# Sample attention of a decoder step: the pages' keys turned by VectorE in 32x32 blocks, scores as nine rounds of four 32-row products

## The chip, the core and the metric

The kernel runs on one core of a Trainium2 chip. Its metric is the device time of one launch in microseconds (us), the median of three runs. A core has TensorE (matrix products out of SBUF into the eight banks of PSUM), VectorE, ScalarE, GpSimd and SyncE; each takes its instructions in order and waits on semaphores for the others. In this kernel SyncE issues nearly all DMAs.

## The reference

One inference step of a two-layer decoder. Each layer has a mixing part (a pooling branch and latent attention, MLA) and a channel part (a gated convolution FFN). It serves two groups with the same weights: a prompt of 512 tokens, and 8 sample sequences of 8 new tokens, each with a past of 2048 tokens that lies in a paged cache. What the change touches is the attention of the samples:

```
past = cache_latent[l][page_table].reshape(n_seq, n_pages * PAGE_SIZE, LATENT)   # 16 pages of 128 rows, 288 wide
keys = jnp.concatenate([past, latent], axis=1)
q_lat = jnp.einsum('bqhn,chn->bqhc', q_nope, lw['w_uk'])
s = einsum('bqhd,bkd->bhqk', [q_lat | q_rope], keys) * ATTN_SCALE    # masked, then softmax -> p
o_lat = einsum('bhqk,bkd->bqhd', p, keys[..., :KV_LORA])
o = jnp.einsum('bqhc,chv->bqhv', o_lat, lw['w_uv'])
```

A cached row is 256 latent values and 32 rope values, 288 in all. With 16 heads and 8 new tokens a sample sequence has 128 query rows, so the scores of one sequence are a product of 128 queries with 2048 + 64 keys over 288 values. All of it is fp32.

## The kernel before

Each layer goes through the projections (weights streamed by DMA and split in two parts by ScalarE and GpSimd), the prompt's attention head by head (16 heads), the sample attention sequence by sequence (b = 0 to 7, `NB`), the output projection and the FFN. Only the sample attention and its neighbours are of interest here.

Pages. `keys_of(b)` on SyncE loads the 16 pages of a sequence, one DMA each, into one of three buffers (`pages[b % 3]`, a key on each partition). Each DMA's address needs a number of the page table, so SyncE does a `value_load` (TENSOR_LOAD and two or three small instructions) ahead of each. `keys_of(0)` stands before the heads; `keys_of(1)` behind `k_asm` of head 15, `keys_of(2)` behind it, and each `keys_of(b)` from b = 3 waits for `spv` of b - 3, the end of the products with the values that read the buffer last.

Scores. The product needs the 288 values on the partitions, so TensorE turns the keys: `turn_rope(b)` (the 32 rope columns of 16 pages, four pages beside each other in the 32-column strips) and `turn_keys(b, g)` (g = 0 to 3, four pages at a time, two blocks of 128). VectorE and ScalarE copy what was turned from PSUM to `ropeT` and `keysT`. `rope_scores(b)` is four products of 32 rows beside each other (each on its own 32 partitions, into banks 0 to 3), `scores(b, g)` two products of 128 rows into bank g, and `new_scores(b)` the 64 new keys. VectorE takes the maximum of each bank as it is done, ScalarE the exponentials of all four banks (`sc`).

Values. `all_values(b)` turns the exponentials with TensorE (`turn_scores`), ScalarE and VectorE copy them to `pT`, and 16 products with the pages and one with the new keys (`newk`) fill bank 7 and raise `spv`. VectorE divides (`olat`, in `outputs(b)`), and TensorE turns that back one sequence later (`turn_output`).

The order is written out by hand: `all_scores(b)`, then `all_values(b - 1)`, so that the exponentials of b run beside the values of b - 1. `all_scores(0)` comes after the last head. The rope part of the queries, `qrs`, lies on partitions 0 to 31, and VectorE copies it to the other three groups of 32 behind head 3.

Of the kernel before, what the change touches and what calls it, by code (L numbers as in the profile page):

```python
# [25 lines left out]
ALU = mybir.AluOpType  # L26
ACT = mybir.ActivationFunctionType
# [56 lines left out]
def build(nc, A, O):  # L84
# [117 lines left out]
    keysT = [at("keysT0", [128, 2, 512], ckv_at), at("keysT1", [128, 2, 512], arena + 18432)]  # L202
    ropeT = [at("ropeT0", [128, 512], ckv_at + 4096), at("ropeT1", [128, 512], arena + 22528)]
# [88 lines left out]
    qlat_p, qlat_ev, qrs_ready = signal("qlat_p", 1), signal("qlat_ev", 1), signal("qrs_ready", 1)  # L292
# [41 lines left out]
    def keys_bank(b, g):  # L334

        return 1 if b == 0 and g == 0 else 4

    def rope_bank(b):

        return 0 if b == 0 else 6  # L340
# [7 lines left out]
    with nc.Block() as block:  # L348
# [3 lines left out]
        def _(sp):  # L352
# [19 lines left out]
            for l in range(DEPTH):  # L372
# [184 lines left out]
        def _(act):  # L557
# [69 lines left out]
            for l in range(DEPTH):  # L627
# [184 lines left out]
                def exponentials(b):  # L812
# [5 lines left out]
                    nc.scalar.activation(sc[:, 0:PAST], PS[:, 0:4, :].rearrange("p a b -> p (a b)"), ACT.Exp,  # L818
# [5 lines left out]
                def turned_scores(b):  # L824
                    for g in (0, 2):
# [3 lines left out]
                for b in range(NB):  # L829
                    keys(b, 0)  # L830
                    if b != 1:
                        keys(b, 1)
                    else:
                        act.wait_ge(newk_T.sem, newk_T.at(l, 1))
                        nc.scalar.activation(newk[:], PS[0:TS, 7, 0:KVL], ACT.Copy).then_inc(newk_ev.sem, 1)
                        keys(b, 1)
# [178 lines left out]
        def _(dve):  # L1015
# [105 lines left out]
            for l in range(DEPTH):  # L1121
# [1105 lines left out]
```

## Time and profile before

| | us |
|---|---|
| median of 3 runs | 2255.96 |
| lowest, highest | 2255.33, 2258.66 |
| the profiled execution | 2255.74 |
| its span | 2254.0 |
| TensorE busy | 2210.7 (98%) |
| VectorE busy | 1170.6 (52%) |
| ScalarE busy | 874.9 (39%) |
| GpSimd busy | 655.1 (29%) |

The profile is of one execution. A span of the trace counts from its first to its last instruction, and times in rows count from its start. In a row of instructions, `x8` counts records; an fp32 product is two records (two passes over its columns), a turn of 128x128 is one. PE is TensorE's products, PEld its weight loads, DVE is VectorE, ACT is ScalarE, POOL is GpSimd, and SPq is SyncE's issuing of DMAs. "Idle before" is the time an engine sat still ahead of a group and who released it.

### The profile page before, as it was taken

The page shows a single profiled execution, that of the slowest core. Times are in us where ns is not written, and L with a number is a line of the kernel's source. Part 1 is how long each engine was busy: PE and PEld are TensorE (multiplying, and loading weights), DVE is VectorE, ACT ScalarE, POOL GpSimd, SP SyncE. Part 2 cuts the span into 40 slices and gives each one's busy share as a digit, 9 for nine tenths or more (in the row PEclk, how much of TensorE's full clock was granted, in tenths as well). Part 3 has the DMA queues.
Part 4 walks back from the last instruction along what each step waited for, and adds up shares of the span by engine and source line. Part 5 has one row for each costly group of instructions (what it writes and reads, how often), then busy time and mean ns, then how long its engine had stood idle before and what let it go on. Part 6 is the DMA issues. An engine that isn't in the chain of part 4 may idle for free.

```text
span 2254.0 us, 42639 instructions
## 1 busy us (share of the span) xinstructions
PE 2210.7 (98%) x16239; PEld 1981.8 (88%) x16239; DVE 1170.6 (52%) x1831; ACT 874.9 (39%) x1815; POOL 655.1 (29%) x316
## 2 busy tenths in 40 slices
PE   7999999999999999999999999999999999999998
PEld 5899997667789999999988999966677999999998
DVE  4443753844346666651153717457443476666433
ACT  4223225832234555541132332366322355555322
POOL 0223433400022333333322334342000323333332
PEclk9999999999999999999999999999999999999999
DMA  9554332033333222235545333212332422222332
GB/s 302 170 145 100 85 85 66 19 109 108 85 130 91 79 84 84 84 109 167 173 126 176 83 97 83 79 43 63 97 108 57 156 70 83 79 80 83 87 85 84
DMA packets 338278, 230.69 MB, mean 102 GB/s; under 512 B 62732, under 2 KB 321605, under 8 KB 338140
## 3 DMA queue, kind: packets, MB, share of 16 engines
q1 hardware_dynamic: 336594, 226.37, 35.1%
q10 hardware_dynamic: 1546, 2.43, 0.4%
q8 instruction: 92, 1.51, 0.3%
q14 instruction: 46, 0.38, 0.1%
HBM read 223.15 MB, written 5.60 MB: 101 GB/s over the span
## 4 chain that ended last, share of the span: by engine, by line
PE 96%; DVE 2%; ACT 1%; DMA 0%; issue 0%; DVEq 0%; SPq 0%; ACTq 0%
PE PS L1550 62%; PE PS L1518 7%; PE PS L2000 5%; PE PS L2047 5%; PE PS L1912 3%; PE PS L1833 2%; PE PS L1646 2%; PE PS L1594 2%; PE PS L1936 2%; PE PS L1567 1%; PE PS L1889 1%; PE PS L1994 1%; PE PS L1950 1%; PE PS L2076 0%; DMA rows_in<-x_sample 0%
## 5 line engine op out<-in xcount | busy, mean ns | idle before, releaser
L975 POOL TENSOR_TENSOR wlo<-raw,whi 128x1024 fp32r<-128x1024 f32 (+1 forms) x248 | 586.0, 2363 | 1493.5 <-ACT whi L563 1493.5
L1550 PE MATMUL PS<-h_hi,whi 128*128 128x288 f32 x2496 | 740.7, 297 | 1.2 <-issue 1.0
L1550 PE MATMUL PS<-h_hi,wlo 128*128 128x288 f32 x2496 | 737.1, 295 | 0.0
L1550 PE MATMUL PS<-h_lo,whi 128*128 128x288 f32 x2496 | 737.0, 295 | 0.0
L563 ACT ACTIVATE whi<-raw 128x1024 fp32r<-128x1024 f32 (+1 forms) x252 | 258.4, 1025 | 919.6 <-PE PS L1550 823.5
L1550 PEld LDWEIGHTS PS<-h_hi,whi 128*128 128x128 f32 x2496 | 470.9, 189 | 9.4 <-issue 8.8
L1550 PEld LDWEIGHTS PS<-h_lo,whi 128*128 128x128 f32 x2496 | 471.0, 189 | 0.2
L1550 PEld LDWEIGHTS PS<-h_hi,wlo 128*128 128x128 f32 x2496 | 470.5, 188 | 0.0
L1452 DVE TENSOR_SCALAR conv<-zext,convp 128x592 f32<-128x592 f32 x88 | 153.6, 1746 | 132.5 <-ACTq L894 132.1
L1550 PE MATMUL PS<-act_hi,whi 128*128 128x288 f32 x704 | 209.9, 298 | 0.0
L1550 PE MATMUL PS<-act_hi,wlo 128*128 128x288 f32 x704 | 207.8, 295 | 0.0
L1550 PE MATMUL PS<-act_lo,whi 128*128 128x288 f32 x704 | 207.7, 295 | 0.0
L1550 PEld LDWEIGHTS PS<-act_hi,whi 128*128 128x128 f32 x704 | 132.8, 189 | 5.5 <-issue 5.4
L1550 PEld LDWEIGHTS PS<-act_lo,whi 128*128 128x128 f32 x704 | 132.9, 189 | 0.0
L1550 PEld LDWEIGHTS PS<-act_hi,wlo 128*128 128x128 f32 x704 | 132.7, 189 | 0.0
L2000 PE MATMUL PS<-keysT,qlat 128*128 128x512 f32 x256 | 122.1, 599 | 0.0
L2047 PE MATMUL PS<-pages,pT 128*128 128x256 f32 x512 | 117.0, 382 | 1.6 <-ACT olatT L809 1.6
L2047 PEld LDWEIGHTS PS<-pages,pT 128*128 128x128 f32 x512 | 94.7, 190 | 15.2 <-ACT olatT L809 2.1
L1115 DVE SCALAR_TENSOR_TENSOR x<-PS,mod,x 128x288 f32<-128x288 f32 x32 | 16.6, 518 | 171.4 <-PE PS L1550 162.1
L803 ACT ACTIVATE keysT<-PS 128x512 f32<-128x512 f32 x64 | 38.2, 597 | 138.9 <-PE PS L1518 138.7
L1044 DVE TENSOR_TENSOR sumsq<-sumsq,tmp 128x576 f32<-128x576 f32 x30 | 49.0, 1633 | 80.1 <-ACT tmp L936 64.7
L1454 DVE SCALAR_TENSOR_TENSOR conv<-zext,convp,conv 128x592 f32<-128x592 f32 x88 | 77.8, 884 | 14.7 <-issue 14.1
(288 smaller groups left out, 3410.8 us busy)
## 6 DMA issues: line engine op xcount, KB each, us to landing
raw<-w_up SPq DMA_DIRECT2D x88, 512.0 KB, 3.8
pages<-cache_latent SPq DMA_DIRECT2D x256, 144.0 KB, 2.1
raw<-w_in SPq DMA_DIRECT2D x64, 512.0 KB, 4.0
ada_ring<-w_ada SPq DMA_DIRECT2D x41, 512.0 KB, 4.9
raw<-w_down SPq DMA_DIRECT2D x32, 512.0 KB, 3.9
ada_next<-w_ada SPq DMA_DIRECT2D x17, 512.0 KB, 4.0
ada_first<-w_ada SPq DMA_DIRECT2D x16, 512.0 KB, 10.4
raw<-w_out SPq DMA_DIRECT2D x16, 512.0 KB, 4.5
```

The lines of the kernel that those rows point to most:

```text
L563: nc.scalar.activation(whi[:, slot, 0:width(u)], raw[:, slot, 0:width(u)], ACT.Copy).then_inc(hi_ready.sem, 1)
L975: nc.gpsimd.tensor_tensor(wlo[:, slot, 0:n], raw[:, slot, 0:n], whi[:, slot, 0:n].bitcast(F32), ALU.subtract).then_inc(lo_ready.sem, 1)
L1044: v.tensor_tensor(sumsq[:], sumsq[:], tmp[:, s, :], ALU.add).then_inc(sq_used.sem, 1)
L1452: v.tensor_scalar(c, zext[:, s, 2:ZE], convp[:, 1, bass.ds(f, 1)], convp[:, 1, bass.ds(f + 2 * KF, 1)], ALU.mult, ALU.add)
L1454: v.scalar_tensor_tensor(c, zext[:, s, 1:ZE - 1], convp[:, 0, bass.ds(f + 2 * KF, 1)], c, ALU.mult, ALU.add)
L1518: return nc.tensor.transpose(out, src, ident[0:k, 0:k])
L1550: r = mm(PS[0:m, 2 * (j % pairs) + half, 0:HT], w, o[:, k0 + k, half * HT:half * HT + HT], start=(first and k == 0 and part is whi and o i ...
L1594: r = mm(PS[:, 2 * s + half, 0:HT], part[:, s, 128 * k:128 * k + 128], o[:, k, half * HT:half * HT + HT], start=k == 0 and part is whi and ...
L1646: o = mm(PS[32 * j:32 * j + 32, 4 + r % 2, 0:256], cond[:, k, :], src[:, 256 * j:256 * j + 256], start=k == 0, stop=k == KD - 1)
L1912: mm(PS[:, qb, 0:128 * (qb + 1)], q96[:, s, 128 * qb:128 * qb + 128], k96[:, s, 0:128 * (qb + 1)], start=True, stop=True).then_inc(qk.sem, 1)
L2000: r = mm(PS[:, g, :], query(qlat[:, c], b), keysT[g % 2][:, c, :], start=False, stop=c == KC - 1)
L2047: mm(PS[:, 7, 0:KVL], pT[:, j, :], pages[b % 3][:, j, 0:KVL], start=j == 0, stop=False)
```

## The change

TensorE no longer turns the pages' keys. VectorE does, with transposes of 32x32 blocks from SBUF to SBUF: `turned_keys(b, chunks)` takes one of nine chunks of 32 values (`NT` = 9) over all 16 pages, 512 columns, and writes it to one of four places of `keysT` (`RING`). In such a piece the partitions 32r to 32r + 31 hold the chunk's 32 values for the keys 32r to 32r + 31 of every page.

A round of `scores(b, chunks)` is then four products of 32 rows, one on each group of 32 partitions, into banks 0 to 3; nine rounds add up the 288 values. Each group needs the queries' 32 values of that chunk on its own partitions, so `queries_of(b)` on SyncE copies `qlat` to `qrep` with 16 DMAs from SBUF to SBUF for each sequence (32 partitions x 2 x 128 values each), and `qrs` is copied to the other groups with 3 DMAs in place of VectorE's three copies. The 16 DMAs stand ahead of `keys_of(b)` from b = 3, and those of b = 1 and 2 both ahead of `keys_of(1)`.

VectorE turns the first four chunks of b + 1 after the maximum of b (now one reduction over the four banks), and ahead of `output(b - 1)`. ScalarE no longer copies keys, and copies three of the four groups of `pT` where it copied two. The exponentials read the banks in another order, so that `sc` has the keys in the order of the pages. Eight of the nine rounds of b = 0 move in front of the turn of head 15's probabilities.

```diff
...
-    keysT = [at("keysT0", [128, 2, 512], ckv_at), at("keysT1", [128, 2, 512], arena + 18432)]
-    ropeT = [at("ropeT0", [128, 512], ckv_at + 4096), at("ropeT1", [128, 512], arena + 22528)]
+    NT, RING = LAT // 32, 4
+    keysT = at("keysT", [128, RING, 512], ckv_at)
+    qrep = [at(f"qrep{i}", [128, NT - 1, 128], o) for i, o in enumerate((work + 5120, q_at + 18432, q_at + 22528))]
...
+                def queries_of(b):
+                    slot, _ = query_slot(b)
+                    for r in range(4):
+                        for k in range(4):
+                            sp.dma_start(qrep[slot][32 * r:32 * r + 32].rearrange("p (c k) n -> p c k n", c=KC)[:, :, k, :],
+                                         qlat[32 * k:32 * k + 32, :, b].rearrange("p c h s -> p c (h s)")).then_inc(qrep_in[slot].sem, 16)
                 keys_of(0)
-                sp.wait_ge(qlat_p.sem, qlat_p.at(l, 1))
+                sp.wait_ge(qrs_own.sem, qrs_own.at(l, 1))
+                for r in range(1, 4):
+                    sp.dma_start(qrs[32 * r:32 * r + 32].rearrange("p b h s -> p (b h s)"), qrs[0:DR].rearrange("p b h s -> p (b h s)")).then_inc(qrs_in.sem, 16)
+                sp.wait_ge(qlat_ev.sem, qlat_ev.at(l, 1))
+                queries_of(0)
                 sp.wait_ge(k_asm.sem, k_asm.at(l, NH))
+                queries_of(1)
+                queries_of(2)
                 keys_of(1)
                 sp.wait_ge(pv.sem, pv.at(l, NH // 2))
...
                 for b in range(3, NB):
                     sp.wait_ge(spv.sem, spv.at(l, b - 2))
+                    sp.wait_ge(multiplied.sem, multiplied.at(l, NT * (b - 1)))
+                    queries_of(b)
                     keys_of(b)
...
+                    else:
+                        act.wait_ge(pv.sem, pv.at(l, NH // 2))
+                    nc.scalar.activation(sc[:, 0:PAST].rearrange("p (j a i) -> p a j i", j=NPG, a=4), PS[:, 0:4, :].rearrange("p a (j i) -> p a j i", j=NPG), ACT.Exp,
...
-                    for g in (0, 2):
+                    for g in range(3):
                         act.wait_ge(spt_p.sem, spt_p.at(l, 5 * b + g + 1))
                         nc.scalar.activation(pT[:, 4 * g:4 * g + 4, :].rearrange("p a b -> p (a b)"), PS[:, 4 + g, :], ACT.Copy).then_inc(spt_a.sem, 1)
...
+                def turned_keys(b, chunks):
+                    for c in chunks:
+                        n, d = NT * b + c, (c - 1) % NT
+                        if c == 0:
+                            for g in range(4):
+                                dve.wait_ge(pages_in[b % 3][g].sem, pages_in[b % 3][g].at(l, 16 * 4 * (b // 3 + 1)))
+                        if n >= RING:
+                            dve.wait_ge(multiplied.sem, multiplied.at(l, n - RING + 1))
+                        v.transpose(keysT[:, n % RING, :].rearrange("p (j i) -> p j i", j=NPG), pages[b % 3][:, :, 32 * d:32 * d + 32]).then_inc(turned.sem, 1)
                 for h in range(NH):
                     maxima(h)
+                    if h == NH - 1:
+                        turned_keys(0, range(RING))
                     if h >= 3 and h % 2 == 1:
                         out_pair(h // 2 - 1)
                     normalised(h)
-                    if h == 3:
-                        for j in range(1, 4):
-                            last = v.tensor_copy(qrs[32 * j:32 * j + 32], qrs[0:DR])
-                        last.then_inc(qrs_ready.sem, 1)
...
+                def maximum(b):
                     o = 16 + 16 * (b % 2)
-                    if b > 0:
-                        rope_keys(b)
-                        keys(b, 0)
-                    keys(b, 1)
-                    maximum(b, 0)
-                    keys(b, 2)
-                    maximum(b, 1)
-                    keys(b, 3)
-                    maximum(b, 2)
-                    new_scores(b)
-                    maximum(b, 3)
-                    v.drain()
-                    v.tensor_reduce(softm[:, o + 5:o + 6], softm[:, o:o + 5], AX.X, ALU.max)
+                    dve.wait_ge(multiplied.sem, multiplied.at(l, NT * (b + 1)))
+                    v.tensor_reduce(softm[:, o:o + 1], PS[:, 0:4, :].rearrange("p a b -> p (a b)"), AX.X, ALU.max)
+                    v.drain()
+                    v.tensor_tensor(softm[:, o + 5:o + 6], softm[:, o:o + 1], softm[:, o + 1:o + 2], ALU.max)
...
                 for b in range(NB):
-                    scores(b)
+                    turned_keys(b, range(RING, NT))
+                    new_scores(b)
+                    maximum(b)
+                    if b == 0:
+                        out_pair(NH // 2 - 1)
+                        v.drain()
+                    else:
+                        turned_scores(b - 1)
+                        denominator(b - 1)
+                    if b + 1 < NB:
+                        turned_keys(b + 1, range(RING))
                     v.tensor_tensor(gate_b[:, b, 0:TP], gate_b[:, b, 0:TP], uext[:, b, 0:TP], ALU.add)
                     if b > 0:
-                        outputs(b - 1)
-                outputs(NB - 1)
+                        output(b - 1)
+                turned_scores(NB - 1)
+                denominator(NB - 1)
+                output(NB - 1)
...
+                def scores(b, chunks):
+                    slot, use_of = query_slot(b)
+                    for c in chunks:
+                        if c == 0:
+                            pe.wait_ge(qrep_in[slot].sem, qrep_in[slot].at(l, 16 * 16 * (use_of + 1)))
+                            if b == 0:
+                                pe.wait_ge(qrs_in.sem, qrs_in.at(l, 3 * 16))
+                                pe.wait_ge(expd.sem, expd.at(l, 4 * NH))
+                            else:
+                                pe.wait_ge(s_exp.sem, s_exp.at(l, b))
+                        n = NT * b + c
+                        pe.wait_ge(turned.sem, turned.at(l, n + 1))
+                        for r in range(4):
+                            rows = slice(32 * r, 32 * r + 32)
+                            q = query(qrs[rows], b) if c == 0 else qrep[slot][rows, c - 1, :]
+                            last = mm(PS[:, r, :], q, keysT[rows, n % RING, :], start=c == 0, stop=c == NT - 1)
+                        last.then_inc(multiplied.sem, 1)
...
+                        scores(0, range(6))
+                        new_scores(0)
+                        scores(0, range(6, NT - 1))
+                        pe.wait_ge(new_ev.sem, new_ev.at(l, 1))
                     turn_probs(h)
-                turn_keys(0, 0)
+                scores(0, range(NT - 1, NT))
...
                 def all_scores(b):
-                    if b > 0:
-                        turn_rope(b)
-                        turn_keys(b, 0)
                     if b == 1:
                         pe.wait_ge(o_done.sem, o_done.at(l, NH // 2))
                         for c in range(KC):
                             r = turn(PS[0:TS, 7, 128 * c:128 * c + 128], ckv[:, c, TP:T], 128)
                         r.then_inc(newk_T.sem, 1)
-                    rope_scores(b)
-                    turn_keys(b, 1)
-                    scores(b, 0)
+                    scores(b, range(2))
                     if b >= 2:
                         turn_output(b - 2)
-                    turn_keys(b, 2)
-                    scores(b, 1)
-                    turn_keys(b, 3)
-                    scores(b, 2)
+                    scores(b, range(2, 6))
                     new_scores(b)
-                    scores(b, 3)
+                    scores(b, range(6, NT))
...
-                pe.wait_ge(qrs_ready.sem, qrs_ready.at(l, 1))
-                all_scores(0)
...
```

TensorE's queue at the start of the scores of sequence 2 (`pages_137` is its buffer) before; waits stand in brackets:

```order
2331 L1950 MATMUL PS<-ident,pages_137 32x128 [waits pages_in21,pages_in22,pages_in20,pages_in23,new_ev,spt_a]
2332 L1950 MATMUL PS<-ident,pages_137 32x128 x15
2333 L1518 MATMUL PS<-ident,pages_137 128x128 [waits kt_a,kt_d,spt_d,spt_a]
2334 L1518 MATMUL PS<-ident,pages_137 128x128 x7
2335 L1994 MATMUL PS<-ropeT_140,qrs 128x512 [waits s_exp,kt_d]
2336 L1994 MATMUL PS<-ropeT_140,qrs 128x512 x3
2337 L1518 MATMUL PS<-ident,pages_137 128x128 [waits kt_d,kt_a]
2338 L1518 MATMUL PS<-ident,pages_137 128x128 x7
2339 L2000 MATMUL PS<-keysT_138,qlat 128x512 [waits kt_d,kt_a]
2340 L2000 MATMUL PS<-keysT_138,qlat 128x512
```

and of the change, at the same place (`qrep_141` holds the queries of sequence 2):

```order
2329 L1964 MATMUL PS<-keysT,qrs 128x512 [waits turned,s_exp,qrep_in2]
2330 L1964 MATMUL PS<-keysT,qrs 128x512 x3
2331 L1964 MATMUL PS<-keysT,qrep_141 128x512 [waits turned]
2332 L1964 MATMUL PS<-keysT,qrep_141 128x512 x3
2333 L1523 MATMUL PS<-ident,olat 128x128 [waits so_d]
2334 L1523 MATMUL PS<-ident,olat 128x128
2335 L1964 MATMUL PS<-keysT,qrep_141 128x512 [waits turned]
```

The turns of pages are gone; each round waits for VectorE's piece (`turned`), and the turn of `olat` stands behind the second round.

SyncE's queue between the pages of sequence 2 and those of sequence 3 (buffer `pages_135`) before:

```order
301 L491 DMA wuv<-w_uv 128x2x1024 [waits q_asm]
302 L478 TENSOR_LOAD tab [waits spv]
303 L478 ISA x2
304 L479 ISA
305 L479 DMA pages_135<-cache_latent 128x288
```

and of the change:

```order
308 L504 DMA wuv<-w_uv 128x2x1024 [waits q_asm]
309 L488 DMA qrep_140<-qlat 32x2x128 [waits multiplied,spv]
310 L488 DMA qrep_140<-qlat 32x2x128 x15
311 L477 TENSOR_LOAD tab
312 L477 ISA x2
```

The 16 copies of the queries stand between the wait for `spv` and the first page.

VectorE's queue after the maximum of a sequence in the change (`pages_135` is the buffer of the next one):

```order
425 L1387 RECIPROCAL softm<-softm 128x1
426 L1350 STREAM_TRANSPOSE keysT<-pages_135 128x512 [waits pages_in03,pages_in02,multiplied,pages_in01,pages_in00]
427 L1350 STREAM_TRANSPOSE keysT<-pages_135 128x512 [waits multiplied] x3
428 L1407 TENSOR_TENSOR gate_b<-gate_b,uext 128x512
429 L1393 TENSOR_SCALAR olat<-PS,softm 128x256 [waits spv]
430 L1350 STREAM_TRANSPOSE keysT<-pages_135 128x512 [waits multiplied] x5
```

The wait for all four page semaphores now stands on VectorE, ahead of the writing of `olat`.

## Rows read from the trace of the kernel before

**Rows 1.** The page, part 4: the chain that ended last, by engine.
```profile
PE 96%; DVE 2%; ACT 1%; DMA 0%; issue 0%; DVEq 0%; SPq 0%; ACTq 0%
```

**Rows 2.** Timeline, TensorE, scores of one sequence: start us, length us, engine, line, operation.
```profile
567.61 1.08 PE L1950 MATMUL PS<-ident,pages 128*32 128x128 f32 x32
568.62 1.09 PE L1518 MATMUL PS<-ident,pages 128*128 128x128 f32 x8
569.64 1.14 PE L1994 MATMUL PS<-ropeT,qrs 32*128 32x512 f32 x8
571.64 1.88 PE L2000 MATMUL PS<-keysT,qlat 128*128 128x512 f32 x4
573.36 0.38 PE L1518 MATMUL PS<-ident,olat 128*128 128x128 f32 x2
...
578.76 0.55 PE L2005 MATMUL PS<-ckv,qlat 128*128 128x64 f32 x4
...
581.43 1.47 PE L1518 MATMUL PS<-ident,sc 128*128 128x128 f32 x12
```

**Rows 3.** Timeline, TensorE: first instruction after the values of 0 and 6, last of 7.
```profile
497.26 1.08 PE L1950 MATMUL PS<-ident,pages 128*32 128x128 f32 x32
...
637.95 1.53 PE L1518 MATMUL PS<-ident,sc 128*128 128x128 f32 x12
...
648.16 0.70 PE L2076 MATMUL PS<-newk,pT 64*128 64x256 f32 x2
```

**Rows 4.** Timeline, SyncE's DMAs, and the page's median from issue to landing.
```profile
445.92 33.40 SPq L479 DMA_DIRECT2D pages<-cache_latent  x31
...
521.52 17.05 SPq L479 DMA_DIRECT2D pages<-cache_latent  x16
...
pages<-cache_latent SPq DMA_DIRECT2D x256, 144.0 KB, 2.1
```

**Rows 5.** Timeline, SyncE: two of fourteen small DMAs in a row.
```profile
2114.76 0.31 SPq L529 DMA_DIRECT2D o_conv_p<-conv_rows  x1
...
2119.32 0.32 SPq L529 DMA_DIRECT2D o_conv_s<-conv_rows  x1
```

**Rows 6.** The chain in order of time, heads 3 to 7; VectorE's copies of `qrs`.
```profile
394.63 2.40 PE PS L1936 x16
...
405.80 2.38 PE PS L1936 x16
...
414.83 2.30 PE PS L1936 x16
...
399.53 2.40 DVE L1341 COPY qrs<-qrs 32x1024 f32<-32x1024 f32 x3
```

**Rows 7.** Groups of VectorE and ScalarE: count | busy us, mean ns of one.
```profile
L1288 DVE STREAM_SHUFFLE tmp<-qr 128x576 f32<-128x576 f32 x8 | 6.5, 818 | 0.1
...
L1360 DVE TENSOR_REDUCE softm<-PS 128x1 f32<-128x512 f32 x64 | 44.3, 692 | 71.4 <-PE PS L2000 71.4
...
L818 ACT ACTIVATE sc<-PS,softm 128x2048 f32<-128x2048 f32 x16 | 31.5, 1968 | 36.3 <-PE PS L1518 26.3 <-DVE softm L1385 9.9
```

**Rows 8.** Windows: stretch, busy us by engine (records), granted clock, DMA.
```profile
381.00:384.00 3.00, 1.34 (x6) 0.44 (x4) 2.17 (x9) 2.97 (x8) 2.49 (x4) 1.00 0.54 149
386.00:387.00 1.00, 1.00 (x2) 0.18 (x1) 0.84 (x4) 0.15 (x1) 0.00 (x0) 0.50 0.28 60
388.00:389.00 1.00, 1.00 (x9) 1.00 (x8) 0.83 (x5) 1.00 (x4) 0.94 (x1) 0.71 0.12 32
```

**Rows 9.** The four-product round of sequence 0: timeline, then windows of its line.
```profile
460.55 1.14 PE L1994 MATMUL PS<-ropeT,qrs 32*128 32x512 f32 x8
461.62 1.09 PE L1518 MATMUL PS<-ident,pages 128*128 128x128 f32 x8
...
460.90:461.00 0.10, 0.10 (x4) 0.00 (x0) 1.00 0.45 161
461.00:461.10 0.10, 0.10 (x7) 0.00 (x0) 1.00 0.26 69
```

More of the change, by code:

```diff
@@ L291, in build @@
     y_ready, q_roped, gated = signal("y_ready", 4), signal("q_roped", 1), signal("gated", KD, 2)
-    qlat_p, qlat_ev, qrs_ready = signal("qlat_p", 1), signal("qlat_ev", 1), signal("qrs_ready", 1)
+    qlat_p, qlat_ev, qrs_own = signal("qlat_p", 1), signal("qlat_ev", 1), signal("qrs_own", 1)
+    qrs_in = signal("qrs_in", 3 * 16)
+    qrep_in = [signal(f"qrep_in{i}", n * 16 * 16) for i, n in enumerate((1, 4, 3))]
     q_asm, k_asm, k_rope = signal("q_asm", NH), signal("k_asm", NH), signal("k_rope", 2)
@@ L332, in ada_at, with query_slot @@
         return range(n, min(n + 2, 5 * KD))
[L334 to L340, printed above, removed]
+    def query_slot(b):
+        return (0, 0) if b == 0 else (1 + (b - 1) % 2, (b - 1) // 2)
     def last_banks(n):
@@ L829, in _ @@
                 for b in range(NB):
-                    keys(b, 0)
-                    if b != 1:
-                        keys(b, 1)
-                    else:
+                    if b == 1:
                         act.wait_ge(newk_T.sem, newk_T.at(l, 1))
                         nc.scalar.activation(newk[:], PS[0:TS, 7, 0:KVL], ACT.Copy).then_inc(newk_ev.sem, 1)
-                        keys(b, 1)
                     if b >= 2:
                         latent_output(b - 2)
-                    keys(b, 2)
-                    keys(b, 3)
                     if b >= 1:
@@ L1938, in pair_values @@
                     r.then_inc(pv.sem, 1)
-                def turn_rope(b):
-                    if b >= 2:
-                        pe.wait_ge(spt_a.sem, spt_a.at(l, 2 * (b - 1)))
-                    if b >= 1:
-                        pe.wait_ge(new_ev.sem, new_ev.at(l, b))
-                    for g in range(4):
-                        pe.wait_ge(pages_in[b % 3][g].sem, pages_in[b % 3][g].at(l, 16 * 4 * (b // 3 + 1)))
-                    for t in range(4):
-                        for g in range(4):
-                            r = mm(PS[32 * g:32 * g + 32, rope_bank(b), 128 * t:128 * t + 128], pages[b % 3][:, 4 * g + t, KVL:LAT], ident[:], start=True, stop=True)
-                    r.then_inc(kt_p.sem, 1)
@@ L1953, in turn_keys, with query @@
-                def turn_keys(b, g):
-                    if b >= 2 and g == 0:
-                        pe.wait_ge(spt_a.sem, spt_a.at(l, 2 * (b - 1)))
-                        pe.wait_ge(spt_d.sem, spt_d.at(l, 3 * (b - 1)))
-                    if b > 0 or g > 0:
-                        pe.wait_ge(kt_a.sem, kt_a.at(l, 4 * b + g))
-                        pe.wait_ge(kt_d.sem, kt_d.at(l, 5 * b + g + (g > 0)))
+                def query(t, b):
+                    return t[:, b].rearrange("p h s -> p (h s)")
@@ L1961, in turn_keys, with new_scores @@
+                def new_scores(b):
+                    if b == 0:
+                        pe.wait_ge(pt_ev.sem, pt_ev.at(l, NH - 1))
                     for c in range(KC):
-                        for j in range(4):
-                            r = turn(PS[:, keys_bank(b, g) + c, 128 * j:128 * j + 128], pages[b % 3][:, 4 * g + j, 128 * c:128 * c + 128], 128)
-                    r.then_inc(kt_p.sem, 1)
+                        mm(PS[:, 6, 0:TS], query(qlat[:, c], b), ckv[:, c, TP:T], start=c == 0, stop=False)
+                    mm(PS[:, 6, 0:TS], query(qrs[0:DR], b), krope[:, TP:T], start=False, stop=True).then_inc(s_new.sem, 1)
```

83 lines of the change are left out of this document (18 added, 65 removed).

## The prediction

> **What bounds the kernel now.** I read the chain that ended last first: 96% of it is TensorE [rows 1], so a microsecond that leaves TensorE's queue is one of time as long as nothing else is late. Then the timeline of one sequence of the sample attention. Its scores start at 567.61 and its successor's turns of exponentials at 581.43, 13.8 us [rows 2]. From sequence 0 to 6 the marks stand at 497.26 and 637.95 [rows 3], 23.45 us a sequence, so 9.6 us go to the values. Sequence 7 ends at 648.16 + 0.70 = 648.86, 10.9 later. TensorE is the pace here. The timeline of SyncE shows how near the next bound is: the 16 page DMAs of a sequence take 17.05 us to issue, one each (17.05 - 0.33) / 15 = 1.115 us, and land 2.1 us after issue [rows 4]. A buffer is free at 520.7 (497.26 + 23.45), the first DMA goes out 0.8 later. SyncE is busy 17.8 of 23.45 us; 5.6 are spare. It is issue that sets this rate: two buffers in a row take the same 1.1 us each (33.40 for 31) and the landing time stays at 2.1.
>
> **TensorE's share.** Of the 13.8 us, the scores proper are 1.07 (the rope round, 569.64 to 570.71), 4 x 1.72 = 6.9 (571.64 to 573.36 is one group), 0.2 for the turn of olat and 0.85 for the new keys [rows 2]. The remaining 4.8 are turns of pages, which go. The scores become nine rounds of four. In the only round that the trace has undisturbed, four records live at 460.9 and the other four join at 461.0, 0.45 us after the start at 460.55, and the next full-width instruction starts at 461.62, after 1.07 [rows 9]. So a round is two passes of 0.43 to 0.45 with four products beside each other, and about 0.2 is the change of form at its end. In a row I take 0.86 a round; there are three stretches of rounds (2, 4 and 3). 9 x 0.86 + 3 x 0.2 = 8.3, and with 0.85 for the new keys 9.2 (call it S), 9.4 with the turn of olat. At 1.07 for every round S is 10.5. The values stay at 9.6. TensorE's work per sequence falls from 23.45 to 19.0, by 4.4 us, which over 16 sequences would be 71 us. That is the gain offered.
>
> The Trainium skill (TensorE: Matmul & The Clock Gate, "Measured speedup vs the span model") gives 3.07 for four 32-row products of 512 columns beside each other, not 4. A round would then be an estimated 4 x 0.86 / 3.07 = 1.12 us, S 10.9. This trace's passes start 0.45 apart, against that rule, but its one round says little of nine.
>
> **VectorE's share.** No row has a transpose. The nearest is the shuffle of 576 columns, 818 ns; less 64 columns at its rate it is 0.7 to 0.75, and a reduction of 512 out of PSUM is 0.69 [rows 7]. Below I bound it by 0.5, above by twice the shuffle, 1.5. I take 0.7, or 0.6 from one to the next. Nine are 5.4 to 6.3 us, against four copies and the rope copy (5 x 0.69) and a copy of pT (0.69) that go; four reductions become one of 2048, some 2.3 us (0.69 + 1536 columns at the 512 per 0.53 us that the rate of these rows leaves). VectorE stays under 15 of 23 us. The maximum comes 2.9 us after the last round, where it came 1.4 after; the exponentials wait for the turns of the previous ones anyway, and at 1.97 us [rows 7] they end well inside the values' 9.6. Nothing there. ScalarE loses four copies and gains one.
>
> One thing on VectorE costs: the first transposes of b + 1 wait for its pages, and the writing of olat is queued behind them, and TensorE's turn of olat behind that. Where the pages are late, TensorE does two rounds (1.9) and waits until 4 transposes, the gate sum and olat are done, about 3: a stall of 1.0.
>
> In the heads VectorE's three copies of qrs (2.40 us) go. The steps of two heads are 11.17 there (394.63 to 405.80) and 9.03 next (405.80 to 414.83) [rows 6]: 2.1 to 2.2 gained per layer, since DMAs do it with 50 us to spare.
>
> **SyncE's share, on which it turns.** 16 DMAs more per sequence. None of before copies SBUF to SBUF, but fourteen small ones in a row go out at (2119.32 - 2114.76) / 13 = 0.35 us [rows 5]. Two bounds: 0.25, below the shortest such row, and 0.45, a page's DMA of 0.33 [rows 4] plus a third. I take 0.35, 5.6 us per sequence, just what was spare. SyncE then needs 5.6 + 17.8 = 23.4, plus 0.1 for the second wait, 23.5 us a sequence, against 23.45 that TensorE needed. The other loop is no shorter: from the end of values b - 3 to the landing of pages b are 0.1 + 5.6 + 0.7 + 16.7 + 2.1 = 25.2 (0.8 + 16.7 + 2.1 = 19.6 before), then 1.0 (wait, one transpose, wait), S with the stall 10.4, values 9.6: 46.2 for two sequences. Before, pages landed 3.9 us ahead of need; now they land 6 us behind TensorE.
>
> **The sum, first layer.** SyncE was let go by k_asm at 445.2 (445.92 less the 0.7 of a table read); now at 443.0 for the heads' 2.2. 32 query DMAs: 454.2. Last page of 1 issued at 454.9 + 16.7, landed 473.7. TensorE is ready at some 468 and starts at 474.7; values of 0 end at 474.7 + 9.2 + 9.6 = 493.5. Pages of 2 land at 491.5, in time. Pages 3 start there; TensorE, done with values 1 at 512.6, waits until 493.5 + 25.2 + 1.0 = 519.7. SyncE paces the rest: 4 x 23.5 to the start of pages 7, 25.2 + 1.0 + 10.4 + 9.6 to the end of values 6, 10.9 to the end: 493.5 + 94.0 + 46.2 + 10.9 = 644.6, 4.3 us under 648.86.
>
> Against it stands the clock. After a stretch in which TensorE sat idle more than half of 3 us (1.34 busy of 3.00) the granted clock was 0.50 at 386 and full again within 389 [rows 8], that is 1.2 in place of 2.4 GHz over some 3.4 us, 1.7 us of work lost. Now there are two waits of 7 us in each layer (ahead of the scores of 1 and 3) and four of some 3. The first delays everything, 1.7; the second 0.9, since SyncE has that much slack against it; at 0.8 each for the four short ones, half low, the pace of 46.2 / 2 rises over 23.5 and about 1.0 more is lost. 4.3 - 3.6 = 0.7 us per layer. Two layers: 1.4 us under the execution's own 2255.74, or 2254.5 to the half microsecond; that execution is 0.22 under the median 2255.96. Forecast: **2255 us**, no change that can be told. Within 0.2% (4.5 us) is what I call the same, about what a measurement of this kernel can tell.
>
> **Rivals.**
> (a) The gain arrives, in part or whole. If the query DMAs go out at 0.1 us, SyncE needs 19.5 and the pages' loop is 42.2, 21.1 a sequence: about 45 us faster, 2210; at 0.25 some 20, 2235; all of TensorE's 4.4 would be 2185. For it: TensorE's queue really is shorter, and 96% of the chain is TensorE. Against it: [rows 5] at 0.35, whatever a DMA's size. 14%.
> (b) Waits for the clock do not lower it, or DMAs go out at 0.33: 2246 to 2249. 10%.
> (c) Slower: every round costs the 1.07 of [rows 9]. S is 10.5, the pages' loop 46.2 + 1.3 = 47.5 and with 0.8 for the clock 24.15 a sequence in place of 23.5. Four such steps are 2.6, the first scores and the last add 1.3 each: 5.2 a layer, 2265. The point from which it decides is 0.95 us a round (S 9.4 or more), since below that SyncE hides it. For it: nine rounds with a wait each. 12%. At the 1.12 of the Trainium skill's section above the same sum is 2268.
> (d) Slower: the transpose at 1.4. Rounds then come at VectorE's pace, S about 12.6: 2287. Against it: the shuffle. 7%.
> (e) Slower: small DMAs on this queue take 0.40 to 0.45, or page DMAs land later behind them. 112 query DMAs of a layer are in SyncE's chain (32, then 5 x 16), each 0.01 us costs 1.1 a layer, 2264 to 2275. 12%.
> That the four products do not run beside each other at all (36 x 0.86 = 31 us of scores) is excluded by [rows 9].
>
> The forecast keeps 45%; its own spread (clock 0 to 3 us more a layer, rates within 0.01) is 2248 to 2264: 30 of the 45 fall within 0.2%, 6 below, 9 above. Below are a, b and 6: 30%. Within: 30%. Above are c, d, e and 9: 40%. The range 2235 to 2280 leaves out most of (a) and (d), some 18%; the forecast's own is 2248 to 2264.
>
> **What would show it.** SyncE without idle time from the third sequence on, its sequence (first page to first page) 23.5 us; 16 small DMAs taking 5.6. TensorE's share below 90% in this phase, with waits on VectorE's transpose ahead of each sequence's scores from 3 on, of about 3 us, and a turn of olat that waits 1 us. Steps from values to values of 23 to 24. Transposes of 0.7 us. Stretches at 0.5 clock behind the waits. It would be wrong if the end of values moves by 19 us a sequence, if SyncE shows gaps, or if rounds are not 0.86 apart.

## The result: 3% slower, and SyncE the pace

| | before | after |
|---|---|---|
| median, us | 2256.68 (4 runs beside it) | 2325.63 (4 runs, 2322.07 to 2327.1) |
| ratio | | 1.0304, 95% interval 1.0291 to 1.0318 |
| span of the profiled execution | 2254.0 | 2324.8 |
| TensorE busy | 2210.7 (98%) | 2168.0 (93%) |

The forecast was 2255, its range 2235 to 2280, and the time lies outside it. Of the cases it is (e), a longer issue time of the small DMAs, but far past the price that (e) had.

The chain that ended last, in the page of the changed kernel, by engine and by line. Before it was 96% TensorE [rows 1]:

```profile
PE 73%; SPq 13%; issue 7%; POOLq 3%; DVE 1%; DMA 1%; ACT 0%; POOL 0%; DVEq 0%; ACTq 0%
PE PS L1555 60%; SPq L488 6%; SPq L477 4%; SPq L478 3%; POOLq L988 2%; PE PS L1599 2%; PE PS L2022 2%; PE PS L1964 2%; PE PS L1523 2%; PE PS L1651 2%; PE PS L1838 2%; PE PS L1572 1%; POOLq L1006 1%; DMA rows_in<-x_sample 0%; DMA pages<-cache_latent 0%
```

The kernel is 3% slower. SyncE's issuing (SPq) holds 13% of the chain now, by three lines: L488 copies the queries, L477 reads the page table, L478 loads a page. The timeline of SyncE in the first layer (start, us, engine and line, what), which answers to [rows 4]:

```profile
440.94 21.40 SPq L488 DMA_DIRECT2D qrep<-qlat  x32
463.14 34.89 SPq L478 DMA_DIRECT2D pages<-cache_latent  x32
498.07 0.43 SPq L504 DMA_DIRECT2D wuv<-w_uv  x1
503.74 10.24 SPq L488 DMA_DIRECT2D qrep<-qlat  x16
514.75 17.08 SPq L478 DMA_DIRECT2D pages<-cache_latent  x16
531.93 11.18 SPq L488 DMA_DIRECT2D qrep<-qlat  x16
543.88 17.23 SPq L478 DMA_DIRECT2D pages<-cache_latent  x16
561.22 10.22 SPq L488 DMA_DIRECT2D qrep<-qlat  x16
...
617.96 10.22 SPq L488 DMA_DIRECT2D qrep<-qlat  x16
```

From 503.74 on each row begins where the last one ends, but for 0.1 us and, ahead of pages, the 0.7 us of a table read: no idle time. Sixteen copies take 10.2 to 11.2 us (0.64 to 0.70 each), and 32 take 21.40, 0.67 each. A sequence is (617.96 - 503.74) / 4 = 28.6 us where TensorE had needed 23.45. Sixteen pages still take some 17.1, as before. The forms of the two copying lines (ns, least/median/most) show that nearly all of it is inside the single instruction (0.60) and not in the gap to the next (0.07):

```profile
L488 SPq DMA_DIRECT2D qrep<-qlat x256: 585/597/1735, 394.9 to 1771.4; - x128
```
```profile
L494 SPq DMA_DIRECT2D qrs<-qrs x6: 584/595/618, 393.0 to 1535.5; - x6
```

The other side is TensorE, in the timeline of the scores of 2 and the start of 3 (in brackets the idle time ahead and who ended it):

```profile
503.64 1.14 PE L1964 MATMUL PS<-keysT,qrs 32*128 32x512 f32 x8
...
505.57 0.44 PE L1523 MATMUL PS<-ident,olat 128*128 128x128 f32 x2
505.93 3.72 PE L1964 MATMUL PS<-keysT,qrep 32*128 32x512 f32 x32
509.58 0.66 PE L1971 MATMUL PS<-ckv,qlat 128*128 128x64 f32 x4
...
513.16 1.53 PE L1523 MATMUL PS<-ident,sc 128*128 128x128 f32 x12
...
522.22 0.69 PE L2048 MATMUL PS<-newk,pT 64*128 64x256 f32 x2
534.73 2.09 PE L1964 MATMUL PS<-keysT,qrs 32*128 32x512 f32 x8 [11.81 <-DVE keysT L1350]
...
545.95 1.53 PE L1523 MATMUL PS<-ident,sc 128*128 128x128 f32 x12
```

Where nothing is late, the scores take 513.16 - 503.64 = 9.5 us and the values 9.7: TensorE's own work is 19.2 us a sequence, so the gain that the change offers is real. But then it waits 11.81 us for keys. There are six such waits in the layer: 17.26, 11.81, 8.29, 6.15, 7.51 and 7.54, ahead of the scores of 1 and of 3 to 7, 58.6 us in all. VectorE, named as the releaser, waited itself (engine, line, what for: us, times, longest), here in both layers:

```profile
DVE keysT L1350 <- DMA pages<-cache_latent: 156.7, 14, 17.0
PE PS L1964 <- DVE keysT L1350: 118.0, 14, 17.4
```

The values of the last sequence end at 681.6, before at 648.86 [rows 3]: 32.8 us later, in a phase in which TensorE has, by an estimate from 23.45 - 19.2 = 4.25 a sequence, some 32 us less to do.

### The profile page after: what moved, and what is told of

The parts are those of the page before. It is cut to its first block, busy times and chain, and to the rows that moved or that the text cites. A ratio compares the mean times of both kernels' runs of the same rounds, so it can differ in the third digit from the quotient of the medians.

```text
span 2324.8 us, 42209 instructions
## 1 busy us (share of the span) xinstructions
PE 2168.0 (93%) x15983; PEld 1936.3 (83%) x15983; DVE 1190.8 (51%) x1825; ACT 843.5 (36%) x1767; POOL 655.1 (28%) x316
## 4 chain that ended last, share of the span: by engine, by line
PE 73%; SPq 13%; issue 7%; POOLq 3%; DVE 1%; DMA 1%; ACT 0%; POOL 0%; DVEq 0%; ACTq 0%
PE PS L1555 60%; SPq L488 6%; SPq L477 4%; SPq L478 3%; POOLq L988 2%; PE PS L1599 2%; PE PS L2022 2%; PE PS L1964 2%; PE PS L1523 2%; PE PS L1651 2%; PE PS L1838 2%; PE PS L1572 1%; POOLq L1006 1%; DMA rows_in<-x_sample 0%; DMA pages<-cache_latent 0%
## 5 line engine op out<-in xcount | busy, mean ns | idle before, releaser
L1350 DVE STREAM_TRANSPOSE keysT<-pages 128x512 f32<-128x512 f32 x144 | 95.7, 694 | 183.2 <-DMA pages<-cache_latent 156.7
L1964 PE MATMUL PS<-keysT,qrs 32*128 32x512 f32 x128 | 29.6, 1009 | 117.6 <-DVE keysT L1350 117.6
L1964 PE MATMUL PS<-keysT,qrep 32*128 32x512 f32 x1024 | 137.5, 651 | 0.3 <-DVE keysT L1350 0.3
L1964 PEld LDWEIGHTS PS<-keysT,qrs 32*128 32x128 f32 x128 | 7.8, 275 | 122.8 <-issue 122.8
L1964 PEld LDWEIGHTS PS<-keysT,qrep 32*128 32x128 f32 x1024 | 69.0, 206 | 45.8 <-issue 33.5
```

Source lines behind the costliest of these rows:

```text
L1350: v.transpose(keysT[:, n % RING, :].rearrange("p (j i) -> p j i", j=NPG), pages[b % 3][:, :, 32 * d:32 * d + 32]).then_inc(turned.sem, 1)
L1964: last = mm(PS[:, r, :], q, keysT[rows, n % RING, :], start=c == 0, stop=c == NT - 1)
```

## The experiments

The edits are shortened: `...` stands for what is left out of a line, `4 x 4` for two loops of four, and `<-` for a DMA from right to left.

The theory after the result: SyncE takes 0.67 us for each copy of the queries, 16 x 0.67 + 17.8 = 28.5 us a sequence, and that alone made the kernel slower. Rivals: the transfers themselves (landing, ports), the order in which SyncE sends them, the rounds or the transposes.

**What a copy costs by its ends.** The kernel before with 20 DMAs more per layer, behind the load of wuv, in five kinds of four: qlat to four groups of 32 partitions in SBUF, DRAM to SBUF, qlat to DRAM, all 128 partitions in SBUF, and the same 32 partitions in SBUF.

```
+for i in range(4): sp.dma_start(spare[32*i:32*i+32, 0:2, :], qlat[0:32, :, i] ...)
+for i in range(4): sp.dma_start(spare[32*i:32*i+32, 2:4, :], A["x_prompt"][0, 32*i:32*i+32, 0:256] ...)
+for i in range(4): sp.dma_start(A["scratch"][l, 32*i:32*i+32, 0:256] ..., qlat[0:32, :, i] ...)
+for i in range(4): sp.dma_start(spare[:, 4+i, :], qlat[:, 0, i] ...)
+for i in range(4): sp.dma_start(spare[0:32, 8+2*i:10+2*i, :], qlat[0:32, :, 4+i] ...)
```

> The kernel before, with 20 small DMAs per layer on SyncE in its idle stretch behind the load of w_uv (17 us between 480 and 497), four of each of five kinds, 32 KB each save the fourth kind (64 KB): from SBUF to SBUF with 32 partitions to each of the four groups; from DRAM to SBUF; from SBUF to DRAM; from SBUF to SBUF with all 128 partitions in one DMA; from SBUF to SBUF within the same 32 partitions. It asks what made the copies of the queries cost SyncE 0.60 us each (21.40 us for 32) where 0.31 was forecast. Theory A (both ends in SBUF cost the issuing engine): kinds 1, 4 and 5 take 0.60, kinds 2 and 3 0.29 to 0.35. Rival B (32 partitions or the offset between partition groups): 1 is 0.60, 4 and 5 are 0.35. Rival C (the piece of 512 bytes, two per partition): 1, 2, 3 and 5 are 0.60, 4 is 0.35. The time should stay at 2256 within 3 us, since the stretch was idle.

The 0.31 there is the length of the instruction in [rows 5]; the forecast itself was 0.35 from one to the next.

Measured 2259.77 in one run (before 2257.82). SyncE's instructions of these five lines, in the order of the kinds:

```profile
L495 SPq DMA_DIRECT2D spare<-qlat x8: 596/602/759, 482.6 to 1592.5; - x8
...
L497 SPq DMA_DIRECT2D spare<-x_prompt x8: 416/421/592, 485.3 to 1594.7; - x8
...
L499 SPq DMA_DIRECT2D scratch<-qlat x8: 577/594/598, 487.3 to 1597.1; - x8
...
L501 SPq DMA_DIRECT2D spare<-qlat x8: 592/599/612, 489.8 to 1599.7; - x8
...
L503 SPq DMA_DIRECT2D spare<-qlat x8: 597/657/1172, 492.4 to 1602.3; - x8
```

From SBUF to SBUF it is 0.60 with other partitions as the end, 0.60 with all 128 in one DMA and 0.66 within the same 32; from DRAM it is 0.42. But to DRAM it was 0.59 too. That both ends lie in SBUF is then not the whole rule, so a second probe changed the sizes: 32 pieces of 512 bytes SBUF to SBUF, 16 of them, 32 pieces of 1 KB, 64 strided pieces from DRAM, and 16 pieces to DRAM.

```
-... the five kinds above
+spare[0:32, i, :] <- qlat[0:32, 0, i]                      spare[0:16, 4+i, :] <- qlat[0:16, 0, i]
+spare[32*i:32*i+32, 8:10, :] <- qlat[0:32, 0, 2*i:2*i+2]   spare[32*i:32*i+32, 10:13:2, :] <- x_prompt, 2 x 128 of 512
+scratch[l, 16*i:16*i+16, 0:128] <- qlat[0:16, 0, i]
```

> The kernel before with twenty DMAs more per layer on SyncE behind the load of wuv, in five kinds of four. The first probe had 0.60 us for each with its source in SBUF, even to DRAM, and 0.42 for one from DRAM, but conv_rows go from SBUF to DRAM at 0.33. Kinds: 32 pieces of 512 bytes SBUF to SBUF; 16 such pieces; 32 pieces of 1 KB; 64 strided pieces of 512 bytes from DRAM; 16 pieces of 512 bytes SBUF to DRAM. If the number of pieces sets the issue time, 16 pieces take 0.33 and the 64 from DRAM 0.60. If the source in SBUF sets it, all but the fourth take 0.60 and that one 0.42.

Measured 2257.12 in one run (before 2256.63).

```profile
L495 SPq DMA_DIRECT2D spare<-qlat x8: 585/592/624, 480.5 to 1589.8; - x8
...
L497 SPq DMA_DIRECT2D spare<-qlat x8: 588/589/590, 483.1 to 1592.3; - x8
...
L499 SPq DMA_DIRECT2D spare<-qlat x8: 589/590/592, 485.6 to 1594.8; - x8
...
L501 SPq DMA_DIRECT2D spare<-x_prompt x8: 420/427/582, 488.2 to 1597.0; - x8
...
L503 SPq DMA_DIRECT2D scratch<-qlat x8: 412/424/1711, 490.2 to 1598.9; - x8
```

From SBUF to SBUF every DMA takes 0.59 us, with 16 pieces, 32, or 1 KB each: neither of the two expected rules holds. With one end in DRAM it is 0.42 here for both directions. What gives 0.59 to the first probe's DRAM copy (64 pieces from two places of each partition) and 0.33 to a page stays open. For this kernel it is enough that none of the six kinds from SBUF to SBUF was cheap.

**The copies alone, in the kernel before.** The same 16 DMAs per sequence at the same places, into memory that nothing reads; TensorE still turns the keys.

```
+copies_of(b): for r, k in 4 x 4: sp.dma_start(spare[b % 2][32*r:32*r+32] ..., qlat[32*k:32*k+32, :, b] ...)
+copies_of(1); copies_of(2)          # ahead of keys_of(1)
+copies_of(b)                        # b = 3 to 7, ahead of keys_of(b)
```

> The kernel before, whole, with the change's 112 copies of queries per layer added at the places where the change issues them (32 ahead of the pages of sequence 1, 16 ahead of the pages of each from 3 on), into memory that nobody reads. Nothing of VectorE's or TensorE's work is changed. Theory (SyncE's issue of the copies sets the pace): a sequence takes 16 x 0.667 + 16 x 1.115 = 28.6 us from the third on, the end of the values of 7 comes 42 to 44 us later per layer, some 2340 us in all. Rival (the time went into VectorE's transposes, the rounds or the waits between those two): 2256 to 2262, since only 5 us of issue per sequence had room.

2344.55 us (2343.38 to 2347.37), ratio 1.0385 (1.0368 to 1.0402). From sequence 3 to 7 the copies stand 28.9 us apart (511.04 to 626.54 for four). The transposes and rounds are not in this kernel, and it is slower than the changed one. So they are not what costs.

**No copies for sequences 3 to 7.** The changed kernel without them; these sequences use old queries, which is the part of the computation left out.

```
-sp.wait_ge(multiplied.sem, multiplied.at(l, NT * (b - 1)))
-queries_of(b)
```

> The changed kernel without the copies of the queries of sequences 3 to 7 (80 of 112 per layer; their scores are computed with the queries that lie in the buffers, so the samples' output is not the reference's). All other work and all other waits stay. Theory (SyncE's issue): from sequence 3 on the pages' loop sets the pace, 20 to 20.5 us a sequence in place of 28.6, and the time is 2233 us, 92 under the change and 23 under the kernel before. Rival (rounds, transposes or clock cost the time): it stays over 2290.

2237.46 us (2237.1 to 2238.85), ratio 0.9912 (0.9895 to 0.9928), 4 us above what was expected. One long wait, of 17.16 us, is left (the others are under 1.6), ahead of the scores of 1, where 32 copies still stand in front of the pages:

```profile
441.57 21.24 SPq L488 DMA_DIRECT2D qrep<-qlat  x32
463.61 35.06 SPq L478 DMA_DIRECT2D pages<-cache_latent  x32
```
```profile
483.62 2.09 PE L1963 MATMUL PS<-keysT,qrs 32*128 32x512 f32 x8 [17.16 <-DVE keysT L1348]
524.79 1.14 PE L1963 MATMUL PS<-keysT,qrs 32*128 32x512 f32 x8 [1.08 <-DVE keysT L1348]
```

**Pages ahead of the copies.** Only the order on SyncE turned.

```
-queries_of(1); queries_of(2); keys_of(1); ...; keys_of(2)
+keys_of(1); queries_of(1); ...; keys_of(2); queries_of(2)
-queries_of(b); keys_of(b)
+keys_of(b); queries_of(b)
```

> The changed kernel with SyncE's order turned: the pages of a sequence are issued ahead of the copies of its queries (pages 1, copies 1, pages 2, copies 2, and from sequence 3 on pages, copies). The same DMAs, the same number. Theory (what counts is the sum of issue times, not what stands first): only the start gains, some 11 us at the first values and 5 to 6 us per layer in the end, since SyncE is busy from the first to the last: 2312 to 2315. Rival (the order is at fault, the copies delay the pages): each sequence gains up to 10 us, under 2270.

2310.76 us (2309.04 to 2312.78), ratio 1.0234 (1.0217 to 1.0252). The order is worth 15 us, from the start of each layer: the scores of 1 begin at 471.79 where they began at 483.09. TensorE now waits for the copies where it waited for the pages, 5.4 to 8.0 us ahead of each sequence, and the pace stays. SyncE's copies begin at 517.74 and 603.24, three sequences apart, 28.5 us each:

```profile
517.74 10.56 SPq L488 DMA_DIRECT2D qrep<-qlat  x16
529.14 16.67 SPq L478 DMA_DIRECT2D pages<-cache_latent  x16
...
603.24 10.22 SPq L488 DMA_DIRECT2D qrep<-qlat  x16
```

**The copies from GpSimd's queue.** GpSimd has nothing to do in this phase. SyncE keeps those of sequence 0.

```
+for b in range(1, NB):              # GpSimd, behind the heads; from b = 3 behind the scores of b - 2
+    for r, k in 4 x 4: nc.gpsimd.dma_start(qrep[slot][32*r:32*r+32] ..., qlat[32*k:32*k+32, :, b] ...)
```

> The changed kernel with the sixteen copies of the queries for sequences 1 to 7 issued from GpSimd's queue; SyncE keeps those of sequence 0 and all pages. Theory (SyncE's issue time sets the pace, the copies themselves are harmless): SyncE then needs 17.8 us a sequence, and the pages' loop of two sequences, 19.6 + 1 + 10 + 9.6 = 40.2, or about 20.3 a sequence, is what is left: 2195 us, and first scores come some 11 us earlier than in the changed kernel. Rival (the copies cost through the transfers or the ports, wherever they are issued): between 2290 and 2326. If GpSimd's own issue is slower than SyncE's (it has none of these here in the trace before), a wait for qrep stands ahead of scores 2 or 3.

2202.24 us (2200.16 to 2206.5), ratio 0.9761 (0.9746 to 0.9776). The same number of the same copies, and 123 us less than the changed kernel. The transfers themselves are not what cost the time. GpSimd's timeline: 16 go out in 8.4 us, and there is no hurry, since it waits for TensorE:

```profile
496.20 8.42 POOL L1009 DMA_DIRECT2D qrep<-qlat  x16 [10.86 <-PE PS L1968]
```

The Trainium skill (DMA: Bandwidth & Descriptors, "Rules for kernel authors") says that spreading DMAs over issuing engines gives no bandwidth, it "only saves sequencer issue time". This run agrees: the bytes are the same, and issue time was what was short.

**Fewer DMAs, through DRAM.** The queries are written once per layer to DRAM by two DMAs and read back by four a sequence, into the same layout. Two things of the order change with it: pages 1 go ahead of queries 1 and 2, and from sequence 3 on the queries go ahead of the wait for the buffer. By itself the first of them is no rival: putting the pages first was worth 15 us above, and this run gains 123. The second was not tried alone.

```
+for c in range(KC): sp.dma_start(A["scratch"][l, :, 128*c:128*c+128] ..., qlat[:, c] ...)
+queries_of(b): for r in range(4): sp.dma_start(qrep[slot][32*r:32*r+32], A["scratch"][l, b] ...)
```

> The changed kernel with the queries written once per layer to a DRAM scratch by two DMAs and read back by four DMAs a sequence in place of sixteen copies; the pages of sequence 0 go out ahead of them, the queries of sequence b ahead of the wait for its buffer. Theory: SyncE needs 4 x 0.4 + 17.8 = 19.5 us a sequence, under the pages' loop of 20.3: 2195 us. Rival: the way through DRAM delays the first queries (2 x 2.1 us and more), then scores of sequence 0 start later and the whole stands at 2205 to 2215. If the issue of DMAs weren't what sets the pace, it would stay over 2290.

2202.81 us (2201.21 to 2205.76), ratio 0.9764 (0.9749 to 0.9779), the same as from GpSimd by another way. Four DMAs take 1.9 us where sixteen took 10.2. Both runs are 7 to 8 us above what was expected: with GpSimd's copies the pages' loop of two sequences takes 41.4 to 42.0 us (the values of 1, 3 and 5 end at 505.54, 547.55 and 588.98) where 40.2 was worked out. In each, TensorE still has waits; here in the timeline of the run through DRAM:

```profile
507.46 2.09 PE L1966 MATMUL PS<-keysT,qrs 32*128 32x512 f32 x8 [1.76 <-DVE keysT L1352]
549.49 1.14 PE L1966 MATMUL PS<-keysT,qrs 32*128 32x512 f32 x8 [1.86 <-DVE keysT L1352]
552.14 0.44 PE L1525 MATMUL PS<-ident,olat 128*128 128x128 f32 x2 [0.66 <-DVE olat L1395]
```

**The copies of qrs alone, in the kernel before.** By DMA in place of VectorE.

```
+sp.dma_start(qrs[32*r:32*r+32] ..., qrs[0:DR] ...)   # r = 1 to 3
-if h == 3: for j in range(1, 4): v.tensor_copy(qrs[32*j:32*j+32], qrs[0:DR])
```

> The kernel before with one part of the change alone: the three copies of qrs to other partitions by DMA instead of twelve VectorE copies. By the step on the heads this saves 2.2 us per layer: 2252. Rival (SyncE or ScalarE sets the heads' time anyway): 2256, no change.

2252.07 us (11 runs), before 2256.63 (15 runs), ratio 0.998 (0.9971 to 0.9989): 4.6 us, 2.3 a layer. The step of two heads that was 11.17 [rows 6] is 8.96 (393.83 to 402.79):

```profile
393.83 2.37 PE L1936 MATMUL PS<-probT,vn 128*64 128x512 f32 x16
...
402.79 2.37 PE L1936 MATMUL PS<-probT,vn 128*64 128x512 f32 x16
```

**Half of the copies on SyncE.** This is the test of the forecast itself. Eight copies take 5.1 to 5.4 us on SyncE, close to the 5.6 that the forecast had for sixteen; the other eight go out from GpSimd. Order and everything else as in the changed kernel.

```
-for k in range(4):
+for k in (range(4) if b == 0 else range(2)):          # SyncE; k = 2, 3 on GpSimd
```

> The changed kernel in its own order, but of the sixteen copies of each sequence from 1 on, eight go out from GpSimd's queue, so that SyncE has eight. Eight copies at 0.667 us are 5.3 us, close to the 5.6 that the forecast had for all sixteen. If the forecast failed in this term alone, its own sum comes true here: 2254 (2246 to 2262). If something else that the copies or the rounds bring was missed too (landings, GpSimd, the clock), it stays above 2265.

2255.82 us (2252.75 to 2256.54, 10 runs), ratio 0.9994 (0.9985 to 1.0004). With the one term near the size that it was given, the forecast's 2255 comes true, and its waits nearly so. Forecast were two of 7 us, ahead of the scores of 1 and 3, and some 3 for the others:

```profile
471.52 2.09 PE L1975 MATMUL PS<-keysT,qrs 32*128 32x512 f32 x8 [5.97 <-DVE keysT L1359]
...
517.57 2.09 PE L1975 MATMUL PS<-keysT,qrs 32*128 32x512 f32 x8 [6.22 <-DVE keysT L1359]
...
540.83 1.14 PE L1975 MATMUL PS<-keysT,qrs 32*128 32x512 f32 x8 [1.30 <-DVE keysT L1359]
...
565.27 2.09 PE L1975 MATMUL PS<-keysT,qrs 32*128 32x512 f32 x8 [4.44 <-DVE keysT L1359]
```

Those of 6 and 7 are 1.14 and 4.69. Behind a long wait the next one is short, and the mean of the four is 2.9. The agreement to the microsecond is in part luck. Ahead of the copies of 5 and of 7 SyncE has gaps of 1.6 and 1.7 us, where the forecast had it busy throughout, and the copies of 3 and of 7 are 95.1 us apart (492.17 to 587.30) where 94.0 was forecast. Against that the copies of 3 start 1.3 us earlier than the 493.5 of the forecast. The values of the first layer end at 646.0.

**Pages from two queues.** On top of the way through DRAM, pages 8 to 15 of sequences 3 to 7 go out from GpSimd beside SyncE's first eight.

```
+for b in range(3, NB):                                  # GpSimd, behind spv of b - 3
+    for j in range(NPG // 2, NPG): page = nc.gpsimd.value_load(tab ...); nc.gpsimd.dma_start(pages[b % 3][:, j, :], ...)
```

> The kernel that sends the queries through DRAM, and for sequences 3 to 7 the second half of the pages goes out from GpSimd's queue. Theory: of the 40 us for two sequences in the pages' loop, 0.7 + 16.7 becomes about 9, so the loop falls to some 31 us, under TensorE's own 38.3, and its waits of 1.9, 1.9 and 0.5 us and the 0.66 at olat go: 5 us a layer, 2193. Rival: GpSimd's DMAs land later or its register loads take over 2 us a page, and it stays at 2203 or rises.

2187.49 us (2185.39 to 2189.66), ratio 0.9692 (0.9676 to 0.9708), 5.5 below what was expected: the fastest of all, 3.1% under the kernel before and 138 us under the changed one. Its chain by engine:

```profile
PE 95%; DVE 2%; ACT 1%; DMA 1%; issue 0%; DVEq 0%; SPq 0%; ACTq 0%
```

and the starts of the scores of sequences 2 and 7; none of the six has a wait ahead:

```profile
487.14 1.14 PE L1977 MATMUL PS<-keysT,qrs 32*128 32x512 f32 x8
...
583.18 1.14 PE L1977 MATMUL PS<-keysT,qrs 32*128 32x512 f32 x8
```

That is (583.18 - 487.14) / 5 = 19.2 us a sequence, TensorE's own work. In this stage nothing is left of what the change offered.

## Why the prediction was wrong

**The step that failed** is "I take 0.35, 5.6 us per sequence", SyncE's share. It measured 0.64 to 0.70 a copy, 0.67 in the stretch of 32, and 10.2 to 11.2 a sequence, outside both bounds (0.25 and 0.45). The mechanism was right, the term was mis-sized. By the forecast's own price (112 copies of a layer in SyncE's chain), 112 x (0.67 - 0.35) = 36 us a layer, and 2255 + 2 x 36 = 2327; measured is 2325.63. In the first layer the end of values was forecast at 644.6, or 648.2 with the clock's 3.6; measured is 681.6. That this term made the miss is shown by the run with half of the copies, which gives 2255.8, and by the copies alone in the kernel before, which put it at 2344.55.

The bound was badly made. The text said that no row had a DMA from SBUF to SBUF, and then took the page's row plus a third as the upper end, for an operation of another kind. The trace of before had slower DMAs on this queue, which were not weighed. They load weights of 512 KB from DRAM; most other loads of that size take 0.37:

```profile
L377 SPq DMA_DIRECT2D ada_late<-w_ada x16: 426/580/1256, 649.3 to 1776.2; - x16
```

With 0.58 as the upper end, the range would have reached to 112 x 0.23 x 2 = 52 us above the forecast, 2307; with the 0.04 or so that lies between two such instructions, some 2315. That is nearer, and still short of 2325.63. A term of which each 0.01 us costs 1.1 us a layer is the last one on which to be narrow.

The other steps:
- TensorE's work, 19.0 a sequence: 19.2 measured. Four rounds take 3.65 us (505.93 to 509.58), 0.91 each, where 0.86 was taken. The stretches of 2, 4 and 3 rounds take 1.93, 3.65 and 2.72 us, together the 8.3 that was forecast, but with the time in each round and not at the end of a stretch. With the new keys and the turn of olat it is 9.5 against 9.4. The rule of the Trainium skill (TensorE: Matmul & The Clock Gate, "Measured speedup vs the span model"), 3.07 times for four products, would make a round an estimated 1.12 us. By 4 x 0.86 / 0.91 it is 3.8 times here, and the measurement decides. Rival (c) is out, since it wanted 0.95 a round or 9.4 for the scores without the turn, and they take 9.15 (9.52 less 0.36).
- The transpose, 0.7: 0.694 (below). Rival (d) is out. The reduction of 2048, 2.3: 2.29.

```profile
L1350 DVE STREAM_TRANSPOSE keysT<-pages 128x512 f32<-128x512 f32 x144 | 95.7, 694 | 183.2 <-DMA pages<-cache_latent 156.7
```

- The stall of 1.0 at the turn of olat: where pages were 6 us late and more, there was none. VectorE wrote olat from 536.85 to 537.32, behind the four transposes, after the scores of 3 had begun at 534.73. The two rounds ahead of the turn take 3.63 us there (534.73 to 538.36), at a granted clock of 0.50, and hide it; at 1.93 they would have ended 0.66 ahead of olat. The stall is there, at 0.66, where pages are just late and the rounds take 1.9 (half of the copies, and through DRAM).

```profile
536.85 0.47 DVE L1393 TENSOR_SCALAR olat<-PS,softm 128x256 f32<-128x256 f32 x1
```

- The heads, 2.1 to 2.2 a layer: 2.3, shown alone.
- The start of the layer: 445.92 in [rows 4] is the second page, for that row has 31 of the 32. The row whole begins 1.1 us earlier, so SyncE was let go at 444.1 and not at 445.2, and every mark of the sum is 1.1 late. In the changed kernel it was let go at 440.9 (443.0 in the forecast). Of these 3.1 us under 444.1 the heads explain 2.3, and the rest stays open.

```profile
444.83 34.48 SPq L479 DMA_DIRECT2D pages<-cache_latent  x32
```

- The clock: during the waits it falls to 0.50, 1.2 GHz, and is still there at the first rounds behind them (window, busy times, granted clock, DMA share, GB/s):

```profile
526.00:528.00 2.00, 0.00 (x0) 0.00 (x0) 0.00 (x0) 0.00 (x0) 0.00 (x0) 0.50 0.50 142
...
536.00:538.00 2.00, 2.00 (x12) 0.47 (x8) 1.94 (x4) 0.00 (x0) 0.00 (x0) 0.50 0.09 20
```

  The scores of 3 take 11.2 us (534.73 to 545.95) in place of 9.5: the 1.7 a wait that was worked out from [rows 8]. Behind the waits ahead of 4 to 7 they take 10.9 to 12.1, 1.4 to 2.6 more, where 0.8 was forecast for shorter ones; while SyncE sets the pace, this costs no time of its own.
- Rival (a) gave 2210 if the copies were nearly free. The run with those of sequences 1 to 7 in GpSimd's queue gave 2202, the one with four larger DMAs a sequence 2203, and 2187 came out for the whole gain (2185 in the text).

## What to carry to other kernels

When work leaves the engine that bounds a kernel, add up the queue that feeds it, one issue at a time; here 16 DMAs of 0.67 us in a queue with 5.6 us to spare turned 70 us of gain into 70 of loss. An operation of which the trace shows no like is bounded at the least by the slowest relative in the trace, not by the nearest plus a margin; here even that falls short, and twenty DMAs in an idle stretch of the kernel before would have given the price. And when a sequencer's issue is the pace, another engine's queue or fewer, larger DMAs give it back, without moving fewer bytes.

## What the runs showed of the hardware

- On SyncE a DMA from SBUF to SBUF held the queue 0.59 to 0.60 us in the median in seven forms out of eight, 0.66 in the other, whether it had 16 or 128 pieces of 512 bytes. For DMAs from DRAM the medians are mostly 0.33 to 0.45, and 0.58 for two groups of loads of `w_ada` in the kernel before.
- GpSimd's queue took less for the same copies: 0.53 (8.41 us for 16), with landing 2.3 us after issue against 1.9 from SyncE.
- Behind TensorE's wait of 11.81 us the granted clock was 0.50 (534.73 to 538), and the first two rounds took 3.6 us in place of 1.9.
- Transfers between SBUF and SBUF, 16 a sequence beside the pages, left the pages' median landing at 2.1 us from SyncE's queue, and 2.2 with the copies in GpSimd's.
